# Encoder trunk in one program: bias lines moved to another DMA queue, two weight splits moved ahead of a norm factor, a third bank for one projection tile, the layers of TensorE written out, another order at the opening

## The reference

```python
for l in range(DEPTH):                                   # DEPTH = 2
    h = x + 0.5 * _swiglu(_rmsnorm(x, ffn1_norm[l]), ffn1_wg[l], ffn1_wu[l], ffn1_wd[l])   # D_FF = 2816
    u = _rmsnorm(h, mix_norm[l])
    p = u @ w_in[l]                                      # 28 tiles of 128 columns
    ret = _retention(...)                                # 4 heads
    dif = _diff_attn(..., rel_bias_table, lam_init)      # 4 heads, logits get a relative-position bias
    h = h + jnp.concatenate([ret, dif], axis=-1) @ w_out[l]
    h = h + 0.5 * _swiglu(_rmsnorm(h, ffn2_norm[l]), ffn2_wg[l], ffn2_wu[l], ffn2_wd[l])
    x = _rmsnorm(h, final_norm[l])
```

## Time and profile before

| | |
|---|---|
| median of 3 runs | 2052.78 us (2052.09 to 2055.35) |
| the profiled execution, whole | 2058.94 us |
| its span (first to last instruction) | 2057.1 us |
| PE busy in it | 1973.4 us, 96% |
| DVE, POOL, ACT busy | 955.8, 871.2, 647.5 us |
| TensorE clock granted, mean | 0.98 of full |

### The profile page before, as it was taken

The page is one execution under the profiler, slowest core; times in us unless marked ns, Lnnn a source line. Parts: engine busy times, 40 slices in busy tenths (PEclk is TensorE's granted clock), DMA queues, the critical chain, the costliest instruction groups (busy, mean ns, idle before and its releaser), DMA issues.

```text
span 2057.1 us, 25192 instructions
## 1 busy us (share of the span) xinstructions
PE 1973.4 (96%) x8654; PEld 1612.3 (78%) x8654; DVE 955.8 (46%) x1095; ACT 647.5 (31%) x909; POOL 871.2 (42%) x388
## 2 busy tenths in 40 slices
PE   8999789999899999999989999999988999999997
PEld 6888578877688788888868888887866887888886
DVE  5424254426856551433554245444285765334145
ACT  4212132435533421222432122224464333222224
POOL 3544154444343544444335444444533335444442
PEclk8999899999999999999999999999999999999999
DMA  3423233222111332232224222223211123322322
GB/s 124 136 93 102 57 113 107 96 94 72 48 66 62 103 102 92 94 100 96 80 72 134 95 99 92 97 82 102 92 58 52 62 82 102 102 92 93 101 89 75
DMA packets 54926, 185.51 MB, mean 90 GB/s; under 512 B 6436, under 2 KB 7972, under 8 KB 54852
## 3 DMA queue, kind: packets, MB, share of 16 engines
q1 hardware_dynamic: 53460, 182.39, 27.0%
q10 hardware_dynamic: 1392, 2.17, 0.3%
HBM read 181.39 MB, written 3.15 MB: 90 GB/s over the span
## 4 chain that ended last, share of the span: by engine, by line
issue 55%; POOL 27%; PE 16%; POOLq 1%; DVE 1%; DMA 0%; ACT 0%; ACTq 0%; DVEq 0%
POOL w_lo L406 25%; PE bank L448 4%; PE bank L449 3%; PE bank L450 3%; POOL a_lo L418 2%; PE pair L448 2%; PE pair L449 2%; PE pair L450 2%; POOLq L404 1%; POOLq L411 0%; DVE a_hi L988 0%; DMA h<-in_x 0%; DVE h L1233 0%; DVE s L986 0%; DVE a_lo L990 0%
## 5 line engine op out<-in xcount | busy, mean ns | idle before, releaser
L406 POOL TENSOR_TENSOR w_lo<-raw,w_hi 128x1024 fp32r<-128x1024 f32 (+1 forms) x344 | 825.2, 2400 | 1127.0 <-ACT w_hi L723 1126.5
L723 ACT ACTIVATE w_hi<-raw 128x1024 fp32r<-128x1024 f32 (+1 forms) x344 | 355.3, 1034 | 706.7 <-PE bank L450 522.0
L448 PE MATMUL bank<-hg_hi,w_hi 128*128 128x512 f32 x1140 | 450.7, 395 | 4.5 <-DVE rg L1202 4.5
L449 PE MATMUL bank<-hg_lo,w_hi 128*128 128x512 f32 x1140 | 445.6, 391 | 0.0
L450 PE MATMUL bank<-hg_hi,w_lo 128*128 128x512 f32 x1140 | 445.2, 391 | 0.0
L448 PE MATMUL bank<-a_hi,w_hi 128*128 128x512 f32 x768 | 301.7, 393 | 24.4 <-POOL w_lo L406 20.0
L449 PE MATMUL bank<-a_lo,w_hi 128*128 128x512 f32 x768 | 299.6, 390 | 0.0
L450 PE MATMUL bank<-a_hi,w_lo 128*128 128x512 f32 x768 | 299.3, 390 | 0.0
L448 PE MATMUL pair<-hg_hi,w_hi 128*128 128x512 f32 x680 | 267.3, 393 | 9.1 <-POOL w_lo L406 9.1
L449 PE MATMUL pair<-hg_lo,w_hi 128*128 128x512 f32 x680 | 266.3, 392 | 0.0
L450 PE MATMUL pair<-hg_hi,w_lo 128*128 128x512 f32 x680 | 266.1, 391 | 0.0
(11 more groups left out here) (181 smaller groups left out, 1553.9 us busy)
## 6 DMA issues: line engine op xcount, KB each, us to landing
raw<-in_w_gu SPq DMA_DIRECT2D x176, 512.0 KB, 3.3
raw<-in_w_dn SPq DMA_DIRECT2D x64, 512.0 KB, 3.3
raw<-in_w_p SPq DMA_DIRECT2D x56, 512.0 KB, 3.3
raw<-in_w_dn SPq DMA_DIRECT2D x32, 384.0 KB, 3.1
raw<-in_w_o SPq DMA_DIRECT2D x16, 512.0 KB, 3.2
h<-in_x ACTq DMA_DIRECT2D x8, 256.0 KB, 6.3
out_y<-h SPq DMA_DIRECT2D x8, 256.0 KB, 2.2
cs<-in_cossin SPq DMA_DIRECT2D x2, 512.0 KB, 4.3
```

The source lines that it names most:

```text
L406: pool.tensor_tensor(w_lo[:, s, 0:tiles, :].rearrange("p a b -> p (a b)"), raw[:, s % RAW, 0:n], w_hi[:, s, 0:tiles, :].rearrange("p a b - ...
L448: pe.matmul(out, w_hi[:, s, k, :], m_hi, start=first, stop=False)
L449: pe.matmul(out, w_hi[:, s, k, :], m_lo, start=False, stop=False)
L723: act.activation(w_hi[:, s, 0:tiles, :].rearrange("p a b -> p (a b)"), raw[:, s % RAW, 0:tiles * P], ACT.Copy).then_inc(hi_done, 1)
```

## The change

The change has six parts.

1. **Bias lines.** Both DMAs leave SP's program and stand in ACT's: the first after the last split of chunk 0, the second after the last of chunk 1, each behind the wait that it had.
2. **Splits ahead of the factor.** At the start of each feed-forward ACT splits the units 4 and 5 (`s` 0 and 1 of the next turn) before it waits for the norm's mean. The first turn of SiLUs then leaves these two out, and is written in front of the loop.
3. **Third bank.** Projection tile 2 goes to `banks[5]` and waits for no `proj_free`. Tiles 3 and later alternate between banks 0 and 1, and wait for the tile that was in theirs. The output projection takes banks 1 and 0 in the other order.
4. **Layers written out on PE.** `for l in range(DEPTH)` takes the place of the hardware loop, and one `pe.If` becomes a plain `if`.
5. **Order of `first_two`.** All products with `w_hi*hg_hi` of both tiles come first, then those with `w_lo`, then those with `hg_lo`.
6. **Opening.** Blocks 0 and 1 of `h` and the small gain are loaded by SP, ahead of its weights. ACT loads blocks 2 to 7, and the tables after `hg_hi`. Unit 1 is split after block 3. The squares from block 2 on wait until all of `hg_lo` is there. PE has 16 instead of 12 matmuls on constants at the start, and 3 more ahead of each of the first 6 real ones.

The diff, cut to its core:

```diff
-WARM_UP = 12
+SP_X = 2
+WARM_UP = 16
+BETWEEN = 3
-        proj = [banks[0], banks[1]]
-        out_banks = [banks[0], banks[1], banks[4], banks[5]]
+        proj = [banks[0], banks[1], banks[5]] + [banks[(t - 1) % 2] for t in range(3, PROJ_TILES)]
+        out_banks = [banks[1], banks[0], banks[4], banks[5]]
...
+            for k in range(SP_X):
+                sp.dma_start(h[:, k, :], x[:, k, :]).then_inc(x_in[k], 16)
+                if k == 0:
+                    sp.dma_start(pr[:, PAR["next_ffn1_g"]], par[DEPTH - 1][:, PAR["next_ffn1_g"]])\
+                        .then_inc(first_gain_in, 16)
...
+            def warm(count):
+                for _i in range(count):
+                    pe.matmul(stat[:, 0:P], ones[:, :], ones[:, :], start=True, stop=True)
...
+                for s in range(2):
+                    pe.wait_ge(hi_done, at(hi_done, l, u + s + 1))
+                    for k in range(EARLY):
+                        if s == 0:
+                            tile_hi(k)
+                            if busy:
+                                busy(BETWEEN)
+                        pe.matmul(outs[s], w_hi[:, s, k, :], hg_hi[:, k, :], start=k == 0, stop=False)
+                for s in range(2):
+                    pe.wait_ge(lo_done, at(lo_done, l, u + s + 1 + RAW))
+                    for k in range(EARLY):
+                        pe.matmul(outs[s], w_lo[:, s, k, :], hg_hi[:, k, :], start=False, stop=False)
+                for s in range(2):
+                    for k in range(EARLY):
+                        if s == 0:
+                            tile(k)
+                        pe.matmul(outs[s], w_hi[:, s, k, :], hg_lo[:, k, :], start=False, stop=False)
...
-                        pe.wait_ge(proj_free, at(proj_free, l, t - 1))
-                        last = product(proj[t % 2], s, hg_hi, hg_lo, KD)
+                        if t >= 3:
+                            pe.wait_ge(proj_free, at(proj_free, l, t - 2 if t < 5 else t - 1))
+                        last = product(proj[t], s, hg_hi, hg_lo, KD)
...
-            with pe.Fori(0, DEPTH) as l:
+            for l in range(DEPTH):
...
+                    if c == 0:
+                        for s in range(2):
+                            split(l, s, UT, (u0 + s + AHEAD) // RAW, (gu_done, 2 * j0 + s + 1))
...
+                    if c == 0:
+                        silus(0, next_split(0), 2)
+                    with act.Fori(int(c == 0), n // 2 - 1) as i:
+                        silus(i, next_split(i))
...
+                        if f == 0 and c < 2 and k == KD - 1:
+                            with act.If(l < 1):
+                                bias_step(c)
...
-            for k in range(KD):
+            for k in range(SP_X, KD):
                 act.dma_start(h[:, k, :], x[:, k, :]).then_inc(x_in[k], 16)
...
+                if k == FIRST_X:
+                    split(0, 1, UT, 0)
...
             for k in range(KD):
+                if k == 2:
+                    act.wait_ge(hg_ready, at(hg_ready, 0, KD))
```

67 lines of the change are left out of this document (25 added, 42 removed).

## The result

The changed kernel takes 2019.92 us (median of 4 runs, 2019.79 to 2022.16); the kernel before takes 2054.07 us beside it (median of 4, 2052.09 to 2060.12). The ratio is 0.983, with a 95% interval of 0.9815 to 0.9844. The gain is 34 us where I had said 50, and the time lies 6.9 us above the top of my range (1996 to 2013). The profiled execution took 2019.79 us, span 2017.9.

What follows compares the result with a forecast made beforehand. PE, busy 96% of the span, bounds the kernel by its work, idle time and half clock. Terms 20.0 + 1.7 + 9.1 + 4.5 + 3.05 + 6.3 + 1.3 + 3.7 = 49.7 us; 2052.8 - 49.7 = 2003 us, range 1996 to 2013.

Steps and rivals of the forecast that it cites:

- 1: lines off SP's queue, with its half clock: Chunk 1's down units: PE's 20.0 us wait behind the bias lines goes, plus 1.7 us for the half clock after it.
- 2: two splits ahead: Start of the feed-forwards: PE's waits for `w_lo` of 2.3, 3.5 and twice 1.65 us all go, 9.1 us.
- half clock after 2 to 4: Four half-clock stretches of PE after removed waits, 13.3 us not yet counted, go and give 6.3 us.
- 6: opening: Products 0 and 1: first real matmul stays at 9.65, third tile starts near 24.7; gain taken as 3.7 us.
- first matmul after each of eight waits: PE's first matmul after each of eight waits is 0.16 us longer; without the waits 1.3 us is gained.
- attention steps: No gain counted; their half-clock stretches may shift, so the range allowed some us either way.
- from the profiled time to the median: Whole kernel: the median lay 6.2 us below the profiled execution; the gain was subtracted from that median, 2052.8 us.
- rival A: Bias lines and weight loads keep one order on the four engines, part 1's 21.7 us come back: 2025 us; chance 0.10.
- B: Feed-forward starts: the norm chain takes the place of `w_lo`, PE waits for DVE's line 983; 2009 us, chance 0.07.
- C: The opening stays at half clock, so its 3.7 us gain becomes -2.4; 2009 us, chance 0.08.
- D: Layer border: written-out layers do not remove the gap, 3.05 + 1.6 us come back; 2008 us, chance 0.03.
- E: PE's longer program stalls on instruction supply, slower than before from 11 stalls on, 2073 us with 15; chance 0.03.

Runs made afterwards that it cites:

- eight-DMA run: Changed kernel with the first bias DMA cut into eight, all issued one after the other on ACT's queue; 2026.49 us, ratio 0.986.
- two-halves run: Changed kernel with the first bias DMA cut into two halves, the second issued behind the third down unit of chunk 1; 2009.05 us, ratio 0.978.
- run from 128 partitions: Changed kernel with the bias lines written to 128 partitions instead of 4, the DMA writing the same 512 rows from there; 2009.76 us, ratio 0.979.
- run with 34 constants: Changed kernel with 34 instead of 16 matmuls on constants at the start of the opening; 2019.48 us, ratio 0.983.

## Why the prediction missed

By its own steps, in us; what was found is from the first traces of the two kernels or from the run that undid the part:

| step | forecast | found |
|---|---|---|
| 1: lines off SP's queue, with its half clock | 21.7 | 11.7 in the traces, 12.5 in the runs |
| 2: two splits ahead | 9.1 | all waits gone, 8.8 |
| 3: third bank | 4.5 | all gone, 4.7 |
| 4: layers written out | 3.05 | all gone, 2.96 |
| half clock after 2 to 4 | 6.3 | gone |
| 6: opening | 3.7 | 0.6 |
| first matmul after each of eight waits | 1.3 | 0.8 (seven waits gone, 0.08 to 0.16 each) |
| attention steps | 0 | 2.2 gained (half clock 3.8 less, waits 1.6 more) |
| from the profiled time to the median | 6.2 | 0.1 in the kernel after |

**The step that failed by most** is in part 1: "If the two queues take turns on an engine, a load has 8 packets there and waits for 8 of the other kind". I set one turn equal to one row, from the first row on. Such turns did come, between 168 and 174, but only behind a run of about 50 rows of lines, and another run followed. A run makes a hold of 50 x 0.298 = 15 us instead of 2.3, and the measured waits are 13.75 and 17.41 us. The sentence after it, that four slots cover 12.6 us "even if a load is late", was written for one late load. The trace had two holds in a row. PE ran dry for 8.59 us, and 3.0 us at half clock came with it: 10.0 us short. The rows I leant on, with both queues busy in one microsecond, were of loads that lie on all engines, and as I wrote they showed no turns on one engine. I kept a bound of 0 for this part (the upper one, 21.9, should have read 21.7) and one sharp rival (the queues don't part, 2025), but nothing between them, and the truth lay in the middle. The eight-DMA run shows that a run of rows does not end with its DMA; the two-halves run shows that the cover holds for one hold; the run from 128 partitions gives the whole term back. What sets the length of 50 rows stays open.

By the Trainium skill, "DMA: Bandwidth & Descriptors", section "Queues, rings and completion order", an engine goes round its rings at packet borders. The Trainium skill gives a packet there as some 9 to 17 descriptors, at most 64, and I had left that out. The trace agrees in part: the engines do serve both queues in turn, and a run of about 50 rows of 2048 bytes lies above the typical size and below the limit. It does not show that a run is one packet, and the turns in small steps between the runs, and the runs that went across DMAs of 16 rows for each engine, speak against it. The section "Issuing engines are not separate DMA queues" of the same page of the Trainium skill, which I had weighed as a reason for rival A, is borne out as to the engines, which are the same, but not as to the time: with the same DMA on SP's queue, and at its old place, the kernel takes 12.5 us more.

**The opening** failed at its first step. I let the first real product stay at 9.65 "plus or minus 1"; it came at 12.47. Of these 2.8 us, 1.55 are the first weights, which are issued behind three more loads on SP's queue (PE's first work after the wait came at 11.20; I had counted 1.4 us for the loads and set it against ACT's earlier start). The other 1.27 are the constants ahead of the first real product, which I had counted behind it, at half clock. The rest up to 3.1 is half clock in the blocks. More would not have come of it, though, since I had looked at PE alone. DVE's sum of squares ends at 32.54 where it ended at 29.42 before (26.15 + 3.27), because POOL runs a second subtraction beside it, which is part 2's doing (with part 2 undone those two additions take 3.26 us again). With the third tile at 25.5, as forecast, its statistic would have been due 5.45 us later (34.07 - 28.62), at 31.0, and would have waited for DVE; the run with 34 constants shows this wait. And the second trace of the kernel before, with a short stretch of half clock, has its opening done 4.1 us sooner than the changed kernel (30.01 against 34.07; in the traces of the other runs with this opening it came between 33.10 and 34.18). On such an execution part 6 is a loss.

**From one execution to the median.** I worked every term out on an execution of 2058.9 us and took the sum off a median that lies 6.2 lower. That execution was one of the high ones of its kind. The other trace of this kernel has 5.5 us less of half clock, and some of what it lacks I had counted as gained; that the same holds for the median execution is likely (their granted clock is 0.983 against 0.980) but has no trace. From profile to profile the forecast was 2009.2, and 2019.8 was measured. So 10.6 of the 16.9 us are the mechanism (10.0 + 3.1 - 2.2 = 10.9 by the table), and 6.2 are this. It was luck, too, that the attention steps gave 2.2 us, for which I had no reason. My range allowed for half-clock stretches that come and go in the opening and the attention steps; the place where they counted was the step to the median.

**The rivals.** A (queues do not part) came half true: 10 of its 21.7. B did not come about at any of the four feed-forwards, nor C as written, since the clock was full from 16.3 on. D and E are excluded by the layer border and by PE's waits in the written-out layers, none of which is for "issue".

## What to carry over

A DMA whose source lies on a few partitions uses only a few DMA engines, and everything that has a part on those engines waits for it; spread the source before you look for a better queue to put it on. When two queues share an engine, price a hold by the longest run that one of them can have, and ask whether the buffers cover two such holds one behind the other, since the second finds them empty. Work out terms on the same execution from which the total is taken, and put down separately what of it (here the half clock, 12 us at work more or less) another execution would not have.

## What the runs showed of the hardware

- A DMA of 512 rows of 2048 bytes from 4 partitions took 40 us at 0.298 us a row and engine; from 128 partitions 3 us, at 0.085 us. So not only the number of engines differs (by 4) but also the time of a row (by 3.5). I have no row that says why.
- Two queues on one engine took turns in an uneven way: about 50 rows of one alone (203 packets on four engines from 152 to 168.5), then rows of both mixed (68 and 58 from 168 to 174), then a run again (191 from 175 to 190.3). Cutting the DMA in eight did not shorten the runs.
- Issuing is not always cheap: the same DMA took 0.81 us on SP's queue and 1.25 us on ACT's, 0.61 us when spread, and eight pieces of it held ACT for 20.67 us.
- The same program with nearly the same sum of waits (75 and 73 us) was at half clock (1.2 GHz) for 41 and for 53 us of work. Its times here went from 2051.5 to 2060.2 us. The four runs of the changed kernel lay closer together (2019.79 to 2022.16).
- One addition of 128x512 on VectorE took 0.69 us, and 2.5 to 2.7 us beside a subtraction of 128x1024 on GpSimd.
- What is gained ahead of a long wait can be lost in the half clock behind it: of 2.1 us gained in the opening 1.54 came to the wait at 189, which took 0.27; the longer half clock took 1.03, and at 360 us 0.17 was left. In the kernels without that wait a gain of 1.07 us was whole at 350 us.
